# A hybrid decoder trunk on one core: small tensors laid down first, large SBUF buffers at multiples of 512 bytes

## The chip, the cores and the metric

One core of one Trainium2 chip runs the whole program. The metric is the device time of one execution in microseconds; lower is better. One execution was also taken with the hardware profiler, and its rows are read below.

## The reference

```python
D_MODEL, SEQ, DEPTH, D_FF = 1024, 512, 2, 4096
def hybrid_layer(x, g_mix, w_in, w_a, w_b, w_o, g_ffn, w_up, w_down):
    proj = rmsnorm(x, g_mix) @ w_in       # 1024 x 9728
    qa, ka, va, qr, kr, vr, gr, ga, gb = jnp.split(proj, SPLIT_POINTS, axis=-1)
    ...   # rotary; three groups of windowed attention with dilation 1, 4, 16, 8 heads of 64 each
    wts = jax.nn.softmax(jnp.stack(lses, axis=0), axis=0)
    y_a = (sum over the groups of wts * outs) @ w_a
    ret = retention(qr, kr, vr)           # 4 heads, keys 128, values 256, decay per head
    y_b = (silu(gr) * rms-normed ret) @ w_b
    x = x + (sigmoid(ga) * y_a + sigmoid(gb) * y_b) @ w_o
    x = x + square(relu(rmsnorm(x, g_ffn) @ w_up)) @ w_down
    return x
```

Two such layers and a last RMSNorm; everything is float32, batch 1.

## The kernel before, in words

**Layout.** Activations lie transposed: 128 features on the partitions, the 512 positions along the free dimension, so `x` is 128 x 8 x 512. Weights come as units of 128 x 2048 float32 (1 MB), two buffers of each kind.

**Three products.** A float32 product is made of three matmuls in the fp32r format. Each operand is split into a high part (a cast) and a low part (the difference): high x high, high x low, low x high, all summed in one PSUM bank (`three`, L1073 to L1077). The moving operand of these, 512 columns of 4 bytes, is the activation (`h_hi`, `h_lo`; `z_hi`, `z_lo`; `m_hi`, `m_lo`; `y_hi`, `y_lo`; in the MLP's second half `u_hi`, `u_lo`, which are `z_hi`, `z_lo` by another name, L159). The weights are the stationary operand. For the values the roles are turned round: the activations are stationary and the weights move, 512 columns at L1124 to L1126 (groups 1 and 2 read `h` with a step of 4, `by_residue`), 256 columns at L1234 to L1236.

**Who splits.** SyncE loads `w_raw` (L305), ScalarE casts it to `w_hi` (L393), VectorE subtracts to `w_lo` (L683), in halves of 1024 columns. TensorE waits for the count of `lo_done`. A unit of weights feeds 48 matmuls.

**Order of a layer.** Values of the three attention groups (six units, 288 matmuls a layer); then a loop over four pairs of heads; in each, three units of queries and keys with rotary (ACT copies out, POOL multiplies by the cosines into `rcos`, L663; DVE shuffles, multiplies and adds, L766 to L779), then twelve steps in which TensorE puts a slice of a projection between the small float32 matmuls of attention and retention: `scores` (L1161), `turn` (L1171), `values` (L1184), `st` (L1197), `ret` (L1210). At the end of a pair DVE makes `z`: `silu` (L822, L827), the square root on ACT (L544), a reciprocal (L856) and two products (L861, L864); its next instructions are the next pair's `w_lo`. Then four passes over the gates (L914, L926) with `w_b` and `w_a`, `w_o` in four units, and the MLP in four chunks of four units `w_up` and four units `w_down`. The waits are semaphores, written out by hand on each engine.

**SBUF.** `sb` takes the next free address, rounded up to 32 bytes. Before the kernel's own tensors the partition is in use up to byte 16481. `x`, `h_hi`, `h_lo`, `w_raw`, `w_hi`, `w_lo`, `tables`, `rstd_all`, `decay`, `mask` come first, then the small ones (L105 to L117). Above them, from `zone0` (L120), lie zones that share the same bytes at different times: "P" for the pairs, "G" for gates and merge, "N" for the norms and the MLP, "X" and "Y" for input and output; `at` (L123) places a tensor. `other` (L115) receives the softmax statistics of the other order by DMA in `exchange` (L345 to L358) and is read in `factors` (L882). `nmax` and `den` (L145, L146) are written by `masked` and `exp` and copied into `stats` in `u_copy` (L795).

Of the kernel before, what the change touches and what calls it, by code (L numbers as in the profile page):

```python
# [35 lines left out]
P = 128  # L36
F32 = mybir.dt.float32
# [14 lines left out]
def trunk(nc, a):  # L52
    S = a["x"].shape[1]
    D = a["x"].shape[2]
    DEPTH = a["w_in"].shape[0]
    KT = D // P
    TB = S // P
# [4 lines left out]
    HEADS = 2 * PAIRS  # L62
# [20 lines left out]
    with ExitStack() as ctx:  # L83
        def sb(name, shape, dt):
            return ctx.enter_context(nc.sbuf_tensor(name, shape, dt))
# [5 lines left out]
            return ctx.enter_context(nc.semaphore(name))  # L91


        x = sb("x", [P, KT, S], F32)
        h_hi = sb("h_hi", [P, KT, S], F32R)
        h_lo = sb("h_lo", [P, KT, S], F32R)
# [4 lines left out]
        cosA, sinA, cosR, sinR = (tables[:, i, :] for i in range(4))  # L101
        rstd_all = sb("rstd_all", [P, S], F32)
        decay = sb("decay", [P, S], F32)
        mask = sb("mask", [P, S], F32)
        ident = sb("ident", [P, P], F32)  # L105
        ones = sb("ones", [P, P], F32)
        inv_d = sb("inv_d", [P, 1], F32)
        gains = sb("gains", [P, 2 * DEPTH + 1, KT], F32)
        gain = sb("gain", [P, 2, KT], F32)
        std = sb("std", [P, 2 * TB], F32)  # L110
        rstd = sb("rstd", [P, 2 * TB], F32)
        eps = sb("eps", [P, 1], F32)

        stats = sb("stats", [P, 2 * TB, 2, HEADS], F32)
        other = sb("other", [P, 2 * TB, 2, HEADS], F32)  # L115
        tick = sb("tick", [P, 1], F32)
        warm = sb("warm", [P, 1], F32)  # L117


        zone0 = -(-nc.sbuf_base // 64) * 64  # L120
        top = {}

        def at(scope, name, shape, dt):  # L123
            off = top.get(scope, zone0)
            n = 2 if dt == BF16 else 4
            for d in shape[1:]:
                n *= d
            top[scope] = off + -(-n // 32) * 32
            return nc.alloc_sbuf_tensor_at(name, shape, dt, offset=off)
# [12 lines left out]
        swp = at("P", "swp", [P, S], F32)  # L142
        rcos = at("P", "rcos", [P, S], F32)
        silu = at("P", "silu", [P, 2, S], F32)
        nmax = at("P", "nmax", [P, 2 * TB, 2], F32)  # L145
        den = at("P", "den", [P, 2 * TB, 2], F32)  # L146

        m_hi = at("G", "m_hi", [P, KT, S], F32R)
        m_lo = at("G", "m_lo", [P, KT, S], F32R)
# [1228 lines left out]
```

## Time and profile before

| | us |
|---|---|
| median of 3 runs | 2015.46 |
| lowest, highest | 2014.9, 2018.23 |
| the profiled execution | 2016.15 |
| its span | 2014.3 |
| TensorE busy, share of the span | 99% |
| VectorE, ScalarE, GpSimd busy | 55%, 36%, 5% |
| mean busy share of the 16 DMA engines | 27.8% |
| mean granted clock of TensorE | 0.998 |

The span runs from the first to the last instruction of the program. In the rows, PE is TensorE's matmul, PEld its weight load (which overlaps the matmuls), DVE VectorE, ACT ScalarE, POOL GpSimd. A matmul's end is modelled: neighbours overlap in the rows, so the time that one takes in a stream is the distance between two starts.

### The profile page before, as it was taken

The numbers are of one execution on the slowest core, as the hardware profiler recorded it, in microseconds if no ns is written. First come the engines' busy times: TensorE is split into PE (matmuls) and PEld (weight loads), VectorE is DVE, ScalarE is ACT, GpSimd is POOL, SyncE is SP. The second block draws the span as 40 slices with busy tenths as digits, with TensorE's granted clock in tenths as the row PEclk, the third lists the DMA queues.
The fourth block names the chain that finished last, engine by engine and source line by source line (L and its number), as shares of the span: only waits on it lengthen the run. The fifth ranks groups of instructions, "written<-read, shape, count | busy, mean of one in ns | idle before, by whom it ended". The sixth has DMA issues, their size and how long they took to land.

```text
span 2014.3 us, 27151 instructions
## 1 busy us (share of the span) xinstructions
PE 1987.7 (99%) x9640; PEld 1656.1 (82%) x9640; DVE 1108.2 (55%) x1724; ACT 727.5 (36%) x1147; POOL 98.2 (5%) x71
## 2 busy tenths in 40 slices
PE   8999999999999999999999999999999999999999
PEld 7988888888888888888889888888888888888887
DVE  5466574747446635444635574757564565445355
ACT  4143535354223313223322534344432233223233
POOL 0010110200000000000001110202000000000000
PEclk9999999999999999999999999999999999999999
DMA  5321222212223233232333222213133323232321
GB/s 173 106 90 48 83 89 62 89 44 84 94 94 105 84 104 101 87 104 84 105 106 89 63 89 62 89 42 99 44 95 97 111 84 105 84 104 83 104 84 63
DMA packets 202544, 177.63 MB, mean 88 GB/s; under 512 B 8432, under 2 KB 192880, under 8 KB 202224
## 3 DMA queue, kind: packets, MB, share of 16 engines
q1 hardware_dynamic: 202192, 176.51, 27.8%
q8 instruction: 38, 0.62, 0.1%
q10 hardware_dynamic: 288, 0.28, 0.0%
q14 instruction: 26, 0.21, 0.0%
HBM read 174.54 MB, written 2.23 MB: 88 GB/s over the span
## 4 chain that ended last, share of the span: by engine, by line
PE 75%; DVE 14%; issue 7%; ACT 2%; POOL 1%; DVEq 0%; DMA 0%; ACTq 0%; POOLq 0%; SPq 0%
PE pj L1075 19%; PE pj L1077 19%; PE pj L1076 19%; DVE w_lo L683 4%; DVE swp L768 3%; PE yo L1184 2%; DVE swp L766 2%; PE rb L1210 2%; DVE probT L856 1%; PE pj L1234 1%; PE pj L1236 1%; PE pj L1235 1%; PE pt L1171 1%; PE sc L1124 1%; PE sc L1126 1%
## 5 line engine op out<-in xcount | busy, mean ns | idle before, releaser
L1075 PE MATMUL pj<-h_hi,w_hi 128*128 128x512 f32 x1408 | 558.2, 396 | 2.2 <-DVE sA L914 1.6
L1077 PE MATMUL pj<-h_hi,w_lo 128*128 128x512 f32 x1408 | 548.6, 390 | 0.0
L1076 PE MATMUL pj<-h_lo,w_hi 128*128 128x512 f32 x1408 | 548.4, 389 | 0.0
L393 ACT CAST w_hi<-w_raw 128x1024 fp32r<-128x1024 f32 x330 | 329.0, 1045 | 380.1 <-PE pj L1077 286.1
L683 DVE TENSOR_TENSOR w_lo<-w_raw,w_hi 128x1024 fp32r<-128x1024 f32 x330 | 404.4, 1267 | 82.7 <-ACT w_hi L393 82.0
L1075 PEld LDWEIGHTS pj<-h_hi,w_hi 128*128 128x128 f32 x1408 | 264.4, 188 | 61.8 <-DVE w_lo L683 5.5
L1077 PEld LDWEIGHTS pj<-h_hi,w_lo 128*128 128x128 f32 x1408 | 264.3, 188 | 56.1
L1076 PEld LDWEIGHTS pj<-h_lo,w_hi 128*128 128x128 f32 x1408 | 264.5, 188 | 54.9 <-issue 1.8
L1075 PE MATMUL pj<-z_hi,w_hi 128*128 128x512 f32 x640 | 252.6, 395 | 0.6 <-DVE sB L914 0.6
L1077 PE MATMUL pj<-z_hi,w_lo 128*128 128x512 f32 x640 | 252.2, 394 | 0.0
L1076 PE MATMUL pj<-z_lo,w_hi 128*128 128x512 f32 x640 | 252.2, 394 | 0.0
L978 DVE TENSOR_TENSOR x<-pj,x 128x512 f32<-128x512 f32 x80 | 55.2, 691 | 201.4 <-PE pj L1077 201.4
L663 POOL TENSOR_TENSOR rcos<-rot,tables 128x512 f32<-128x512 f32 x64 | 97.7, 1526 | 1307.1 <-ACT rot L465 1175.9
L1075 PEld LDWEIGHTS pj<-z_hi,w_hi 128*128 128x128 f32 x640 | 119.7, 187 | 30.3 <-issue 1.1
L1077 PEld LDWEIGHTS pj<-z_hi,w_lo 128*128 128x128 f32 x640 | 119.7, 187 | 29.8
L1076 PEld LDWEIGHTS pj<-z_lo,w_hi 128*128 128x128 f32 x640 | 119.7, 187 | 29.3
L992 DVE TENSOR_TENSOR relu<-relu,rstd_all 128x512 f32<-128x512 f32 x64 | 44.3, 692 | 90.4 <-ACT relu L607 89.8
L465 ACT COPY rot<-pj 128x512 f32<-128x512 f32 x48 | 28.2, 587 | 182.1 <-PE pj L1077 96.8
L476 ACT ACTIVATE prob<-prob,nmax 128x256 f32<-128x256 f32 (+1 forms) x128 | 62.4, 489 | 66.0 <-DVE nmax L790 65.6
L607 ACT ACTIVATE relu<-pj 128x512 f32<-128x512 f32 x64 | 38.3, 599 | 129.2 <-PE pj L1077 129.2
L1234 PE MATMUL pj<-w_hi,h_hi 128*128 128x256 f32 x256 | 79.4, 310 | 0.0
L790 DVE CUSTOM_DVE_ANT_0 prob<-sc,mask 128x256 f32<-128x256 f32 (+1 forms) x128 | 46.9, 404 | 56.6 <-issue 56.6
(185 smaller groups left out, 2358.1 us busy)
## 6 DMA issues: line engine op xcount, KB each, us to landing
w_raw<-in_w_in SPq DMA_DIRECT2D x152, 512.0 KB, 4.4
w_raw<-in_w_up SPq DMA_DIRECT2D x64, 512.0 KB, 4.4
w_raw<-in_w_down SPq DMA_DIRECT2D x64, 512.0 KB, 4.3
w_raw<-in_w_b SPq DMA_DIRECT2D x16, 512.0 KB, 4.0
w_raw<-in_w_o SPq DMA_DIRECT2D x16, 512.0 KB, 4.0
w_raw<-in_w_a SPq DMA_DIRECT2D x16, 256.0 KB, 3.0
x_nat<-in_x SPq DMA_DIRECT2D x2, 1024.0 KB, 7.0
tables<-in_tables SPq DMA_DIRECT2D x2, 1024.0 KB, 6.8
```

The lines of the kernel that those rows point to most:

```text
L393: nc.scalar.copy(w_hi[s][:, c], raw[s][:, c]).then_inc(hi_done, 1)
L476: nc.scalar.activation(prob[:, c], prob[:, c], ACT.Exp, scale=-1.0, bias=nmax[:, at_, b % 2:b % 2 + 1], accum_out=den[:, at_, b % 2:b % 2 ...
L663: nc.gpsimd.tensor_tensor(rcos[:], rot[:], cosA if u < 3 else cosR, ALU.mult).then_inc(rot_cos, 1)
L683: nc.vector.tensor_tensor(w_lo[s][:, c], raw[s][:, c], w_hi[s][:, c], ALU.subtract).then_inc(lo_done, 1)
L768: nc.vector.tensor_tensor(swp[:], swp[:], sinA if u < GROUPS else sinR, ALU.mult).then_inc(rot_sin, 1)
L790: nc.vector.tensor_tensor_reduce(out=prob[:, c], in0=sc[:, (b % 2) * S + c.start:(b % 2) * S + c.stop], in1=mask[:, c], scale=-(DH ** -0.5 ...
L978: nc.vector.tensor_tensor(x[:, t, :], pj[o][:], x[:, t, :], ALU.add).then_inc(bank_free[o], 1)
L992: nc.vector.tensor_tensor(relu2[:, o, :], relu[:, o, :], rstd_all[:], ALU.mult).then_inc(relu_scaled, 1)
L1075: nc.tensor.matmul(out, w_hi[s][:, wc], acts[0], start=first, stop=False)
L1076: nc.tensor.matmul(out, w_hi[s][:, wc], acts[1], start=False, stop=False)
L1077: return nc.tensor.matmul(out, w_lo[s][:, wc], acts[0], start=False, stop=last)
L1234: nc.tensor.matmul(out, hh, w_hi[sl][:, w], start=(k == 0), stop=False)
```

## The change

The small tensors are allocated first; a filler brings the next address to a multiple of 512; `zone0` is rounded up to 512 instead of 64. `other` is no longer a tensor of its own but a view of `decay`'s first 128 columns. `nmax` and `den` move from the zone "P" to the small tensors. No instruction, wait or order changes on any engine.

```diff
+        ident = sb("ident", [P, P], F32)
+        ones = sb("ones", [P, P], F32)
+        inv_d = sb("inv_d", [P, 1], F32)
+        gains = sb("gains", [P, 2 * DEPTH + 1, KT], F32)
+        gain = sb("gain", [P, 2, KT], F32)
+        std = sb("std", [P, 2 * TB], F32)
+        rstd = sb("rstd", [P, 2 * TB], F32)
+        eps = sb("eps", [P, 1], F32)
+
+        stats = sb("stats", [P, 2 * TB, 2, HEADS], F32)
+        tick = sb("tick", [P, 1], F32)
+        warm = sb("warm", [P, 1], F32)
+        nmax = sb("nmax", [P, 2 * TB, 2], F32)
+        den = sb("den", [P, 2 * TB, 2], F32)
+
+        fill = -nc.sbuf_base % 512
+        if fill:
+            sb("fill", [P, fill // 4], F32)
         x = sb("x", [P, KT, S], F32)
...
         decay = sb("decay", [P, S], F32)
+        other = decay[:, 0:2 * TB * 2 * HEADS].rearrange("p (b w h) -> p b w h", b=2 * TB, w=2)
         mask = sb("mask", [P, S], F32)
-        ident = sb("ident", [P, P], F32)
...
-        other = sb("other", [P, 2 * TB, 2, HEADS], F32)
...
-        zone0 = -(-nc.sbuf_base // 64) * 64
+        zone0 = -(-nc.sbuf_base // 512) * 512
...
-        nmax = at("P", "nmax", [P, 2 * TB, 2], F32)
-        den = at("P", "den", [P, 2 * TB, 2], F32)
```

## Rows read from the trace of the kernel before

**Rows 1.** The page, parts 1 and 2: busy time of each engine, granted clock.
```profile
PE 1987.7 (99%) x9640; PEld 1656.1 (82%) x9640; DVE 1108.2 (55%) x1724; ACT 727.5 (36%) x1147; POOL 98.2 (5%) x71
...
PEclk9999999999999999999999999999999999999999
```

**Rows 2.** Waits of PE: us in total, times, the longest.
```profile
PE sc L1047 <- DMA x_nat<-in_x: 7.2, 1, 7.2
PE rb L1197 <- DVE qkR L779: 5.3, 8, 0.7
```

**Rows 3.** Timeline, PE, moving `h`: start us, duration us, instruction.
```profile
1500.05 0.39 PE L1075 MATMUL pj<-h_hi,w_hi 128*128 128x512 f32 x1
...
1505.04 0.39 PE L1076 MATMUL pj<-h_lo,w_hi 128*128 128x512 f32 x1
```

**Rows 4.** Timeline, PE, moving `z`.
```profile
1505.49 0.39 PE L1075 MATMUL pj<-z_hi,w_hi 128*128 128x512 f32 x1
...
1511.79 0.39 PE L1075 MATMUL pj<-z_hi,w_hi 128*128 128x512 f32 x1
```

**Rows 5.** Groups by line and form: count, busy us, mean ns, idle before.
```profile
L1075 PE MATMUL pj<-h_hi,w_hi 128*128 128x512 f32 x1408 | 558.2, 396 | 2.2 <-DVE sA L914 1.6
...
L1076 PEld LDWEIGHTS pj<-h_lo,w_hi 128*128 128x128 f32 x1408 | 264.5, 188 | 54.9 <-issue 1.8
...
L1075 PE MATMUL pj<-z_hi,w_hi 128*128 128x512 f32 x640 | 252.6, 395 | 0.6 <-DVE sB L914 0.6
...
L1075 PE MATMUL pj<-m_hi,w_hi 128*128 128x512 f32 x128 | 50.4, 394 | 0.0
```

**Rows 6.** Timeline, PE, moving `w` with 256 columns.
```profile
315.90 0.28 PE L1234 MATMUL pj<-w_hi,h_hi 128*128 128x256 f32 x1
...
318.30 0.28 PE L1236 MATMUL pj<-w_hi,h_lo 128*128 128x256 f32 x1
```

**Rows 7.** Windows: stretch, length, PE, PEld, DVE, ACT, POOL busy, clock, DMA share, GB/s.
```profile
670.00:1000.00 330.00, 330.00 (x1436) 268.67 (x1435) 164.68 (x200) 103.27 (x135) 0.00 (x0) 1.00 0.30 96
...
30.40:32.60 2.20, 2.20 (x7) 1.68 (x6) 2.00 (x7) 2.19 (x4) 0.00 (x0) 0.50 0.17 20
```

**Rows 8.** Timeline, PE, group 0's values, in the second stretch of rows 7.
```profile
30.44 0.63 PE L1125 MATMUL sc<-w_lo,h_hi 128*128 128x512 f32 x1
...
32.57 0.63 PE L1124 MATMUL pt<-w_hi,h_hi 128*128 128x512 f32 x1
```

**Rows 9.** Timeline, PE, float32 matmuls of `ret`, starts of two neighbours.
```profile
166.04 0.59 PE L1210 MATMUL rb<-ST,vR 128*128 128x512 f32 x1
...
166.47 0.59 PE L1210 MATMUL rb<-ST,vR 128*128 128x512 f32 x1
```

**Rows 10.** Timeline, PE, values of a group that reads `h` with a step.
```profile
59.81 0.40 PE L1126 MATMUL sc<-w_hi,h_lo 128*128 128x512 f32 x1
...
61.93 0.40 PE L1126 MATMUL yo<-w_hi,h_lo 128*128 128x512 f32 x1
```

**Rows 11.** Timeline, PE, a pair's middle; in brackets the idle time before.
```profile
314.36 1.15 PE L1161 MATMUL sc<-qk 64*128 64x256 f32 x12
...
325.53 1.10 PE L1197 MATMUL rb<-qkR 128*128 128x512 f32 x2 [0.66 <-DVE qkR L779]
```

**Rows 12.** Chain that ended last, a pair's end: start us, us, what.
```profile
356.32 0.70 DVE silu L822
...
368.01 1.17 DVE w_lo L683
```

**Rows 13.** The page, part 6, DMA issues: count, KB each, us to landing.
```profile
x_nat<-in_x SPq DMA_DIRECT2D x2, 1024.0 KB, 7.0
tables<-in_tables SPq DMA_DIRECT2D x2, 1024.0 KB, 6.8
```

**Rows 14.** Groups by line and form, ACT's casts of 512 columns.
```profile
L415 ACT CAST h_hi<-hn 128x512 fp32r<-128x512 f32 x40 | 24.3, 608 | 2.6 <-DVE hn L690 2.0
...
L612 ACT CAST z_hi<-relu 128x512 fp32r<-128x512 f32 x64 | 39.8, 621 | 100.1 <-DVE relu L994 100.1
```

More of the change, by code:

```diff
@@ L103, in trunk @@
         decay = sb("decay", [P, S], F32)
+        other = decay[:, 0:2 * TB * 2 * HEADS].rearrange("p (b w h) -> p b w h", b=2 * TB, w=2)
         mask = sb("mask", [P, S], F32)
-        ident = sb("ident", [P, P], F32)
[L106 to L114, printed above, removed]
-        other = sb("other", [P, 2 * TB, 2, HEADS], F32)
-        tick = sb("tick", [P, 1], F32)
-        warm = sb("warm", [P, 1], F32)
-        zone0 = -(-nc.sbuf_base // 64) * 64
+        zone0 = -(-nc.sbuf_base // 512) * 512
         top = {}
```

## The prediction

> **What bounds the kernel now.** I read the page's first two parts first. TensorE (PE) is busy 99% of the span and its granted clock stays at the top level in every slice [rows 1]; VectorE (DVE) at 55% and ScalarE (ACT) at 36% are far behind. Then the waits of PE: the largest are 7.2 us for the first input and 5.3 us, in eight pieces, for `qkR` [rows 2], and all the others together come to less than 9 us. So the time is the number of matmuls times their spacing, and the question is what sets the spacing.
>
> The busy time can't say it (a pipelined matmul shows 390 ns), so I took starts from the timeline. Three products of one form, 128x512 in fp32r, at the same full clock, differ by where the moving operand lies. In the compiled kernel before, `x` begins at byte 16512 of the partition, 128 above a multiple of 512, and since the sizes of everything down to `mask` are multiples of 512, so do `h_hi`, `h_lo`, `w_hi`, `w_lo`. The small tensors end at 131588, so `zone0` is 131648, 64 above a multiple of 512, and so are `z_hi`, `z_lo`, `m_hi`, `m_lo`, `y_hi`, `y_lo`.
> - Moving `h` (start 128): 22 intervals from 1500.05 to 1505.04 us are 226.8 ns each [rows 3], which is 544 cycles of 2.4 GHz: 512 columns and 32 more.
> - Moving `z` (start 64), the same weights as stationary operand: 27 intervals from 1505.49 to 1511.79 are 233.3 ns each [rows 4]: 560 cycles, 48 more. `m` shows the modelled duration of `z`, 394 and 395 ns [rows 5], and `y` lies as they do.
> - Moving `w_hi`, `w_lo` with 256 columns (start 128): 20 intervals from 315.90 to 318.30 are 120.0 ns each [rows 6]: 288 cycles, again 32 more, at half the length. The extra belongs to the start, not to the length.
>
> A whole stretch bears the two out: 330 us of the MLP, where `h` and `z_hi`, `z_lo` take turns, hold 1436 matmuls, 229.8 ns each, the mean of 226.7 and 233.3 [rows 7].
>
> Both extras follow from one rule: if PE is fed in blocks of 256 bytes (64 columns of 4 bytes), a stream that starts inside a block must take its last block whole. From 64, 2048 bytes end 64 bytes into a block: (2304-64)/4 = 560. From 128: (2304-128)/4 = 544. From 128 with 1024 bytes: (1280-128)/4 = 288. A start on a boundary adds nothing. Two more rows speak for a limit of the supply and not of PE: at the low clock (granted 0.50, 1.2 GHz [rows 7]) five intervals of the 512-column form with `w` at start 128 take 2.13 us, 426 ns or 511 cycles, without an extra [rows 8]; and the fp32 form, which takes two cycles a column, takes 430 ns for 512 columns with `ST` at start 64, 6 cycles over 1024 [rows 9].
>
> **The change part by part.**
> *Large buffers.* After the change the small tensors take 16512 to 18592, the filler 352 bytes, `x` starts at 18944 = 37 x 512 and `zone0` is 131584 = 257 x 512. So every moving operand of the 1-cycle products starts on a boundary. Price of one aligned 512-column matmul: bounds are 213.3 ns (512 cycles) and 240 ns (below, a rival); I take 215.8 ns, 518 cycles, since [rows 9] shows 6 cycles over the columns where the supply can't be the limit. The weight load of 188 ns [rows 5] fits under it.
> The Trainium skill (TensorE: Matmul & The Clock Gate, Back-to-back issue gap) gives 512/2.4 + about 2.5, measured 215.7 ns, for this size in bf16. The rows here are 11 and 18 ns above it; by it the sum would come out as mine.
> Counts: `h` 3 x 1408 = 4224; `z` and `m` 3 x (640+128) [rows 5] and `y` 3 x 64 by the loops, 2496 together.
> - `h`: 4224 x (226.7 - 215.8) = 46.0 us.
> - `z`, `m`, `y`: 2496 x (233.3 - 215.8) = 43.7 us.
> - Values for attention (L1124 to L1126, moving `w`, 576 in all by the loops): the 192 of group 0 save 10.9 ns each, 2.1 us. The 384 of the other groups load `h` with a step of 4; nine intervals take 235.6 ns [rows 10], more than the 226.7 of group 0's kind, so I take that load as their limit and save nothing. Bound: 384 x 19.8 = 7.6 us.
> - 256 columns (L1234 to L1236), 768: 120.0 to 262/2.4 = 109.2, 8.3 us.
> Sum 100.1 us.
>
> *What of it is lost.* Each of the eight pairs has two stretches where DVE, ACT and POOL chains end last, so a faster PE only waits longer. First, from the scores at 314.4 to `st` at 325.5: PE already sits idle 0.66 us for `qkR` [rows 11]; the 48 matmuls of 256 columns beside that chain save 0.52 us that becomes waiting. Second, the end of the pair: `silu` at 356.32, then the sigmoid, the square root, a reciprocal, the products for `z`, and `w_lo` at 368.01 [rows 12]; PE runs the next pair's first unit (48 matmuls) beside it and is about caught up, so another 0.52 us goes. Smaller waits in the attention steps may keep 0.2 more, a guess from these two. So 1.25 us of the 3.65 that a pair could give, 10 us in all, and 1 us at the start and at the gates. In the MLP nothing is lost: a unit of 48 matmuls goes from 11.0 to 10.4 us, DVE is busy there half the time, ACT 31%, the DMA engines 30% [rows 7]. Net 100 - 11 = 89 us.
>
> *DMA.* Landings into `w_raw` move from start 128 to 0. PE never waits for one except `x_nat` at the start [rows 2]. Of two 1 MB transfers, `tables` (start 128) lands in 6.8 us, `x_nat` (start 64) in 7.0 [rows 13]: 0.2 us at most; I take nothing. No DMA is added, none passes another, and no wait is added.
> *ACT and DVE.* The same cast takes 608 ns into `h_hi` and 621 into `z_hi` [rows 14]: a difference of 13 ns under PE's cover, and in the lossy stretches at most some tens of ns per pair. Nothing.
> *`other` inside `decay`, `nmax` and `den` out of the zone.* The same instructions on other addresses. `decay` was last read in the layer's fourth pair, before the exchange, and is loaded again after the next layer's values. Nothing.
>
> The profiled execution took 2016.15 us with a span of 2014.3; the median of the runs is 2015.46. From the median: 2015.5 - 89 = 1926.5, say 1927 us.
>
> **Rivals.**
> *Other floors of the same rule.* No residue at all (213.3 ns): 7680 matmuls save 2.5 ns more, 19 us, of which 2 are lost: 1909 us. A residue of 16 cycles (220 ns, 113.3 for 256 columns): 28.2 + 33.3 + 1.3 + 5.1 = 68, less 7: 1954 us.
> *32 cycles are a fixed cost* and only the 64-byte start costs more. All would run at 226.7: 2496 x 6.7 = 16.6 us, 1999 us. For it: 32 is the least extra that a row shows at full clock. Against: [rows 8].
> *Start addresses don't matter* (the change doesn't do what it says). `z`, `m`, `y` also lie above 131072, so the 16 cycles could be of the place, with 32 fixed: 2015.5 us. The Trainium skill (SBUF — State Buffer, Door 1) says that reads run at full bandwidth with two or more hits in each 16-byte line; all starts here are multiples of 16, so by it nothing would change. Against: no row shows 512 or 518 cycles at full clock, and 560, 544 and 288 come from one formula without a constant.
> *Slower.* The same three rows also fit "extra = columns up to the next boundary, and a start on one pays a full block": 48 at 64, 32 at 128, 64 at 0. Then a matmul takes 576 cycles, 240 ns: 4224 x 13.3 + 2496 x 6.7 + 192 x 13.3 + 384 x 4.4 + 768 x 13.3 = 87 us more, 2103 us. It decides from an aligned spacing of 229 ns on, the mean of today's. Against: it needs a block fetched for nothing.
>
> **Chances.** Forecast 0.60, the floors 213.3 and 220 0.10 each, 226.7 0.07, no effect 0.06, slower 0.07. The range 1905 to 1965 holds the first three with their bounds (values 7.6 us, losses between 4 and 16 us). A change below 0.2%, 4 us, is not told from none here. Faster 0.87, same 0.06, slower 0.07.
>
> **What would show it.** In the profile after: `h` and `z` timelines with one spacing, near 216 ns; 256 columns near 109; a unit of 10.4 us; the MLP stretch some 6% shorter; larger idle times before `qkR`'s matmul and before the second unit of a pair; fp32 products and every DVE and ACT mean as before. Spacings of 226.7 or 240 for `h` would make it wrong, as would an unchanged sum with new idle time in the MLP.

## The result, and the profile after

The changed kernel takes 1998.62 us in the median of 4 runs (1997.93 to 2001.2), against 2015.18 us for the kernel before (the three runs of the table and a fourth, 2014.14): a ratio of 0.9918, with a 95% interval of 0.9901 to 0.9935. It is faster by 16.6 us. Forecast was 1927 with a range of 1905 to 1965; the sign was right, the size was wrong by a factor of five. The rival with 1999 us had a chance of 0.07.

The page of the changed kernel, part 1 and a row of part 6 [rows 1, 13]. All lines of the kernel's body are 4 higher than before.

```profile
PE 1969.5 (99%) x9640; PEld 1656.4 (83%) x9640; DVE 1108.3 (56%) x1724; ACT 727.8 (36%) x1147; POOL 98.0 (5%) x71
...
x_nat<-in_x SPq DMA_DIRECT2D x2, 1024.0 KB, 6.4
```

Its timeline of PE where `h` gives way to `z`, as [rows 3, 4]:

```profile
1492.11 0.39 PE L1079 MATMUL pj<-h_hi,w_hi 128*128 128x512 f32 x1
...
1495.51 0.39 PE L1079 MATMUL pj<-z_hi,w_hi 128*128 128x512 f32 x1
...
1498.91 0.39 PE L1079 MATMUL pj<-z_hi,w_hi 128*128 128x512 f32 x1
```

Fifteen intervals each: 3.40 us and 3.40 us, 226.7 ns. `z` came down from 233.3; `h` did not move at all. The forms that carry the sum [rows 5], and the MLP [rows 7]:

```profile
L1079 PE MATMUL pj<-h_hi,w_hi 128*128 128x512 f32 x1408 | 558.2, 396 | 2.2 <-DVE sA L918 1.6
...
L1079 PE MATMUL pj<-z_hi,w_hi 128*128 128x512 f32 x640 | 249.3, 390 | 0.7 <-DVE sB L918 0.7
```

```profile
670.00:992.00 322.00, 322.00 (x1423) 266.70 (x1422) 162.46 (x197) 101.28 (x131) 0.00 (x0) 1.00 0.30 98
...
1000.50:1003.50 3.00, 3.00 (x9) 2.29 (x8) 0.34 (x2) 1.09 (x1) 0.00 (x0) 0.53 0.02 5
```

`h` has the busy time of before to the tenth. In each layer, from the first matmul that moves `z` to the layer's end (in the second layer to the end of the program), the trace shows 538.1 and 549.3 us before, 530.1 and 540.6 after: 16.7 us, which is 2496 x 6.7 ns. The loops over the pairs take 345.1 and 345.0 before, 345.2 and 345.2 after. The two spans differ by 18.2 us: the 16.7, 0.6 by which PE waits less for `x_nat`, and about 1.7 for a stretch of 3.4 us at the low clock (granted 0.5), of which the execution before has one more than this one; the wait for `w_lo`, which grows from 1.8 to 2.4 us, takes 0.6 of it back.

Where it waits [rows 2]:

```profile
PE sc L1051 <- DMA x_nat<-in_x: 6.6, 1, 6.6
PE rb L1201 <- DVE qkR L783: 5.3, 8, 0.7
```

### The profile page after: what moved, and what is told of

Read it like the earlier page. It is cut to its first block, busy times and chain, and to the rows that moved or that the text cites. A ratio compares the mean times of both kernels' runs of the same rounds, so it can differ in the third digit from the quotient of the medians.

```text
span 1996.1 us, 27151 instructions
## 1 busy us (share of the span) xinstructions
PE 1969.5 (99%) x9640; PEld 1656.4 (83%) x9640; DVE 1108.3 (56%) x1724; ACT 727.8 (36%) x1147; POOL 98.0 (5%) x71
## 4 chain that ended last, share of the span: by engine, by line
PE 75%; DVE 14%; issue 7%; ACT 2%; POOL 1%; DVEq 0%; DMA 0%; ACTq 0%; POOLq 0%; SPq 0%
PE pj L1079 19%; PE pj L1081 19%; PE pj L1080 19%; DVE w_lo L687 4%; DVE swp L772 3%; PE yo L1188 2%; DVE swp L770 2%; PE rb L1214 2%; DVE probT L860 1%; PE pj L1238 1%; PE pj L1240 1%; PE pj L1239 1%; PE pt L1175 1%; PE sc L1128 1%; PE rb L1201 1%
## 5 line engine op out<-in xcount | busy, mean ns | idle before, releaser
L1081 PEld LDWEIGHTS pj<-z_hi,w_lo 128*128 128x128 f32 x640 | 120.2, 188 | 24.9
```

Source lines behind the costliest of these rows:

```text
L1081: return nc.tensor.matmul(out, w_lo[s][:, wc], acts[0], start=False, stop=last)
```

## The experiments

Two theories stood after the result. *Own start*: what counts is where the moving operand starts, in units of 128 bytes; 32 cycles are fixed. *Difference*: what counts is the start of the moving operand minus that of the stationary one. Before, `h` and `w` both lay at 128 and `z` at 64 against `w` at 128; no row had told the two apart.

### Three layouts of the whole kernel

`e1_zone_128`, the kernel before with one line changed:

```diff
-        zone0 = -(-nc.sbuf_base // 64) * 64
+        zone0 = -(-nc.sbuf_base // 128) * 128
```

> The kernel before with one edit: zone0 is rounded up to a multiple of 128 instead of 64, so z, m and y start 128 above a multiple of 512, as the main group does; nothing else moves. Own start (unit 128) and difference of the starts both say: z, m, y at 226.7 ns, 16.6 us less than before, 1998.6 us, the whole gain of the change. If a start at a multiple of 256 or 512 is needed, z, m, y stay at 233.3 and the time at 2015.

2001.55 us, ratio 0.9923 (0.9906 to 0.9939). `z` is back at the busy time that it has in the changed kernel, and at a spacing of 226.7 ns:

```profile
L1075 PE MATMUL pj<-z_hi,w_hi 128*128 128x512 f32 x640 | 249.4, 390 | 0.6 <-DVE sB L914 0.6
```

The gain of the change is this line's: neither 512 nor laying the small tensors down first is needed for it. The median is 2.9 us above the changed kernel's, which goes with the granted clock: three of the four runs have a mean of 0.997, and the one at 0.999 took 1998.52 us. Both theories live.

`e2_all_64`, the changed kernel moved as a whole:

```diff
-        fill = -nc.sbuf_base % 512
+        fill = (64 - nc.sbuf_base) % 512
...
-        zone0 = -(-nc.sbuf_base // 512) * 512
+        zone0 = -(-nc.sbuf_base // 64) * 64
```

> The changed kernel with everything large moved by 64 bytes: main group and zone both start 64 above a multiple of 512. Own start (unit 128): every 1-cycle product pays 16 cycles more than in the changed kernel, h too: 233.3 ns for h, z, m, y, 126.7 for the 256 columns; 16.6 us for z, m, y and 28.2 + 1.3 + 5.1 us for the rest, of which the waits of the pairs take up some 5: about 2045 us. Difference of the two starts: moving and stationary operands agree, so all stay at 226.7 and the time at 1999 us.

1999.57 us, ratio 0.9920 (0.9903 to 0.9936). All starts of large buffers are 64 above a multiple of 512, where `z` had cost 233.3 before, and the rows are those of the changed kernel:

```profile
L1079 PE MATMUL pj<-h_hi,w_hi 128*128 128x512 f32 x1408 | 558.1, 396 | 2.2 <-DVE sA L918 1.6
...
L1079 PE MATMUL pj<-z_hi,w_hi 128*128 128x512 f32 x640 | 249.4, 390 | 0.8 <-DVE sB L918 0.8
```

Own start falls here.

`e3_main_64`, the changed kernel with the same `fill` with 64 and `zone0` rounded up to 128, so that `z` lies 128 above a multiple of 512 and its weights 64:

> The changed kernel with the main group (x, h, w, tables) 64 above a multiple of 512 and the zone 128 above one. Own start (unit 128): h and the moving weights pay 16 cycles more, z, m, y don't: h at 233.3, z at 226.7, about 1999 + 30 = 2029 us. Difference of the starts: h (64) against w (64) stays at 226.7, z (128) against w (64) goes to 233.3, 2015 us.

2007.03 us, ratio 0.9956 (0.9940 to 0.9973), which neither theory had named. `h` stays at 226.7, as the difference says; `z` goes up, but to 229.2 in the mean (232.2, 226.2 and 229.3 ns by the three products) and not to 233.3. So a difference of +64 is not one of -64, and the blocks below give its price.

### Blocks of matmuls by themselves

`m1_starts` and `m2_differences` leave the trunk out: PE runs blocks of 48 or 96 matmuls of one form, all on zeros,

```python
for k in range(N):
    mm = nc.tensor.matmul(ps[0][:, 0:512], W(0, 128, k), M(d, 512, k), start=(k == 0), stop=(k == N - 1))
```

where `W(s, ...)` starts s bytes and `M(d, ...)` d bytes above a multiple of 512.

> The trunk is left out; the output is zeros. TensorE alone runs 31 blocks of 48 matmuls from SBUF into one bank each, every block with another start of the moving or the stationary operand, width or type. Read is the spacing of starts inside a block at full clock. Own start (unit 128): a moving start of 0, 128, 256, 384 gives 226.7 ns for 512 columns of fp32r, one of 16, 32, 64, 96, 192, 320, 448 gives 233.3, whatever the stationary start. Difference of the two starts: 226.7 where both have the same start modulo 128, so also with both at 64 or both at 32, and 233.3 where they differ, so also with moving 0 and stationary 64. The 32 cycles that are left at start 0: if they are paid by each matmul as such, 64 or 32 stationary columns and one stationary tile used again and again still take 226.7; if they are the cost of the stationary columns, 64 columns give 528 cycles, 220.0 ns, and 32 columns 520, 216.7. bf16 with 512 columns: 216 to 220 if the residue is of the 4-byte type, 226.7 if it is of every matmul.

> The trunk is left out; the output is zeros. Blocks of 96 matmuls in fp32r; the stationary operand starts at 0 modulo 512, the moving one at d. Theory: the cost depends on the difference d modulo 256 alone. 512 columns: 544 cycles (226.7 ns) at d = 0 and 256, about 549 at 64, 560 at 32, 96, 128, 192, 224; open is whether 8, 48, 80, 112, 144, 160, 176, 208, 240 lie between or below. If one of them is below 544, a layout with that difference beats both kernels. 256 columns: 288 cycles at 0, 283 at 64. The 32 cycles left at d = 0: if they come from weight reads and moving reads that meet in SBUF, they go (to 512 to 518 cycles, 213 to 216 ns) when the moving operand is one column read again and again (step 0), or the stationary one is; if each fp32r matmul pays them as such, the step 0 blocks stay at 226.7 ns. Stationary operand with a step of 4 (as in the values of groups 1 and 2): 235 ns whatever d, if the load is the limit; else it moves with d.

The mean spacing from the first to the last start of a block, fp32r, 512 columns, 128 stationary ones; where both runs have a value they agree within 0.2 ns, except at 128 (233.4 and 232.4); each block was run once in a run:

| moving minus stationary, bytes | ns | cycles |
|---|---|---|
| 0, 240, 256 | 226.7 to 227.1 | 544 to 545 |
| 64, 320 | 228.8, 229.2 | 549, 550 |
| 16, 80, 112, 176 | 231.1 to 231.7 | 555 to 556 |
| 128, 384 | 232.4 to 233.4 | 558 to 560 |
| 8, 32, 48, 96, 144, 192, 224, 448 | 233.2 to 233.6 | 560 to 561 |
| 160, 208 | 234.2, 234.7 | 562, 563 |
| moving 0, stationary 32, 64, 128, 256 | 233.2, 233.4, 232.5, 226.8 | |
| both 32, both 64, both 128 | 227.5, 227.6, 227.6 | |
| 256 columns: 0, 64, 128, 192 | 119.9, 117.8, 118.7, 113.7 | 288, 283, 285, 273 |
| stationary with a step of 4: 0, 64, 128, 192 | 237.8, 239.9, 239.6, 238.3 | |
| moving: one column, step 0 | 215.8 | 518 |
| stationary: one column, step 0 | 228.9 | 549 |
| bf16, moving 0, 64, 128 | 216 (median) | 518 |

To within 1 ns, only the difference modulo 256 counts, and none of the differences tried is better than 0 for 512 columns and 128 stationary ones. Two things that `m1_starts` expected fell: a difference of 128 costs as much as one of 192 (the period is 256, not 128), and 64 or 32 stationary columns take 229.9 and 231.7 ns, neither 220.0 and 216.7 nor 226.7. One stationary tile used again and again takes 227 ns (median in `m1_starts`; 227.0, with the moving tile repeated too, in `m3_residue`). In the groups of `m2_differences` (count, busy, mean ns; the spacing is (busy - mean)/95), the differences 0, 64 and 192, then one moving column:

```profile
L83 PE MATMUL ps<-mov,sta 128*128 128x512 f32 x96 | 21.9, 389 | 0.0
...
L98 PE MATMUL ps<-mov,sta 128*128 128x512 f32 x96 | 22.1, 391 | 0.0
...
L122 PE MATMUL ps<-mov,sta 128*128 128x512 f32 x96 | 22.6, 394 | 0.0
...
L173 PE MATMUL ps<-mov,sta 128*128 128x512 f32 x96 | 20.9, 379 | 0.0
```

The last row is what I had put as the price of an aligned matmul: 518 cycles. PE can do it; a stream of 512 different columns of 4 bytes didn't, at any of the starts tried.

`m3_residue` asks where the other 26 to 32 cycles come from.

> The trunk is left out; the output is zeros. Blocks of 96 fp32r matmuls about the 32 cycles that stay at difference 0 and go when the moving operand is one column (518 cycles). If they come from how many different addresses the moving stream reads: a run of 4, 8, 16, 64, 128 or 256 columns read again until 512 are made shows from which length they return, and 128 columns read 4 times each stand near 518. If they come from meetings with the weight loads: narrower loads (96, 64, 32 columns) need fewer cycles at some difference, in proportion, and each width has its own best difference. Lengths 320, 384, 448, 480: 352, 417, 480, 512 cycles if the residue is 32 per matmul and no share of the length.

Each of 128 columns read four times in a row: 518 cycles; a run of 4 columns again and again 518, of 8 columns 520; of 64, 128 or 256 columns 544, as the full stream; of 16 columns 581. Narrower stationary operands don't help: over the differences 0, 64, 128, 192, 96 columns take 552, 560, 556, 548 cycles, 64 take 552, 548, 550, 558, and 32 take 554 to 556. That goes against a cost in proportion to the width of the weight load. But each width has its cheapest difference elsewhere, as was expected if the moving stream meets the weight loads; for 96 and 64 columns it isn't 0. Lengths: 352 cycles for 320, 416 for 384, 486 for 448, 520 for 480. So 480 columns cost 40 more than their number and 512 only 32: neither a fixed price nor a share. How many different columns the moving stream reads has a part in it; that it meets the weight loads is argued from the differences, and how stays open.

`m4_low_clock` lets PE stand still before each block; its blocks have 96 matmuls, not the 48 of the text on record.

> The trunk is left out; the output is zeros. TensorE stands still for over 15 us before each of seven blocks of 48 fp32r matmuls, so that each block begins at the low clock. If the extra cycles come from how fast SBUF feeds TensorE at 2.4 GHz, then at 1.2 GHz every difference (0, 64, 128, 192, 32) takes 427 ns for 512 columns and 213 for 256, without an extra; if they are cycles of TensorE, 453 ns at difference 0 and 467 at 192.

The windows of the block with difference 192 (granted clock 0.50, then 1.00), and starts in its timeline:

```profile
157.00:160.00 3.00, 3.00 (x9) 2.32 (x8) 0.00 (x0) 0.00 (x0) 0.00 (x0) 0.50 0.00 0
165.00:175.00 10.00, 10.00 (x45) 8.01 (x44) 0.00 (x0) 0.00 (x0) 0.00 (x0) 1.00 0.01 2
```

```profile
156.33 1.22 PE L107 MATMUL ps<-mov,sta 128*128 128x512 f32 x2 [22.10 <-ACT tick L53]
...
159.48 1.05 PE L107 MATMUL ps<-mov,sta 128*128 128x512 f32 x2
...
163.76 0.63 PE L107 MATMUL ps<-mov,sta 128*128 128x512 f32 x2
...
173.79 0.39 PE L107 MATMUL ps<-mov,sta 128*128 128x512 f32 x1
```

From 156.33 to 159.48 there are seven intervals, the first of 595 ns, the others of 426 to 427; from 163.76 to 173.79 forty-three, 233.3 each. After each block's first intervals, the low clock shows 426 to 427 ns at every difference tried (0, 64, 128, 192, 32) and 213 to 214 for 256 columns (differences 0 and 192): no extra. A cost in PE's own cycles would have been there at either clock; so this is a limit outside them that only the full clock meets, as [rows 8] had suggested.

### Two more differences and a moved weight buffer

> The changed kernel with the zone 64 above a multiple of 512 and the main group at 0, so z, m, y move at a difference of +64 to their weights (before it was -64). Difference theory: 228.8 ns for them as in the blocks, 2496 x 2.2 = 5.4 us more than the changed kernel, 2004 us. A rule of the moving operand's own start (64 costs 16 cycles): 233.3 ns and 2015 us.

```diff
-        zone0 = -(-nc.sbuf_base // 512) * 512
+        zone0 = -(-nc.sbuf_base // 512) * 512 + 64
```

2007.96 us, ratio 0.9958 (0.9941 to 0.9975). `z` lies at 64 as in the kernel before, and yet takes 229.2 ns, with the three values of `e3_main_64`: about 6 us more than the changed kernel. The rest of the 9.3 goes with the low clock: its profiled execution has four stretches at it while PE works, that of the changed kernel one (each has another after PE's last matmul, which costs nothing).

> The changed kernel with the zone 128 above a multiple of 512 and the main group at 0: difference +128. Difference theory: 232.4 ns for z, m, y, 2496 x 5.8 = 14.4 us more than the changed kernel, 2013 us. By its own start, z at 128 cost no more than 226.7 ns in the kernel whose zone and main group both lay at 128: 1999 us.

The same edit with + 128: 2015.58 us, ratio 0.9996 (0.9987 to 1.0006). `z` takes 233.4 to 233.5 ns (the blocks had 233.4 and 232.4), 2496 x 6.7 = 16.7 us: the whole gain is gone, with `z` at the start that cost nothing in `e1_zone_128`. Seventeen intervals of its timeline:

```profile
1509.83 0.40 PE L1081 MATMUL pj<-z_hi,w_lo 128*128 128x512 f32 x1
...
1513.80 0.39 PE L1080 MATMUL pj<-z_lo,w_hi 128*128 128x512 f32 x1
```

> The changed kernel with a pad of 64 bytes between the activations and the weight buffers, the zone at a multiple of 256: all activations start at 0, all weights 64 later (difference -64 modulo 256). Difference theory: h too goes to 233.3 ns: 4224 x 6.7 = 28.2 us and 2496 x 6.7 = 16.6 us more than the changed kernel, the moving weights (difference +64) change by less than 2 us together, the pairs take up 1 to 4 us in their waits: 2039 to 2042 us. Own start of the moving operand: all activations at 0, 1999 us.

```diff
         h_lo = sb("h_lo", [P, KT, S], F32R)
+        sb("pad", [P, 16], F32)
...
-        zone0 = -(-nc.sbuf_base // 512) * 512
+        zone0 = -(-nc.sbuf_base // 256) * 256
```

2040.9 us, ratio 1.0124 (1.0107 to 1.0140): 64 bytes ahead of the weights make the kernel 42.3 us slower than the changed one in the medians, though every activation starts at a multiple of 256. `h` and `z` are both at 233.3 to 233.5 ns. Its groups:

```profile
L1080 PE MATMUL pj<-h_hi,w_hi 128*128 128x512 f32 x1408 | 565.5, 402 | 1.1 <-DVE sA L919 1.1
...
L1080 PE MATMUL pj<-z_hi,w_hi 128*128 128x512 f32 x640 | 252.7, 395 | 0.1
```

A part of the 42.3 is the clock. The profiled executions, both at a mean of 0.999, took 2035.25 and 1997.93 us, 37.3 us apart, and the latter has in it 1.7 us for a low-clock stretch that the other doesn't have. So the layout costs some 39 us, the low edge of what was expected. The products' 45 us are not all seen, since the pairs take up some in their waits, and the other runs, at 0.996 and 0.997, carry more low clock.

### A layout from the table

The table has 113.7 ns for 256 columns at a difference of 192. `e7_values_192` gives just these products that difference. ACT and DVE write this unit's `w_hi` and `w_lo` 48 columns (192 bytes) later, in buffers made longer for it, with all large buffers at multiples of 256; PE reads them there (one line of the edit):

```diff
-                                w = slice(k * 256, k * 256 + 256)
+                                w = slice(48 + k * 256, 48 + k * 256 + 256)
```

> The changed kernel unchanged, beside the next one on the same chip: 1998 to 2001 us; its runs differ from each other by the stretches at the low clock, some 1.7 us each.

> The changed kernel; the weights of the retention's values (the 768 products of 256 columns, in which the weights move and h stands still) are written 192 bytes later in their buffers, which grow by 256 bytes; everything large starts at a multiple of 256. Difference theory: 113.7 ns instead of 119.9 for the 256 columns, as in the blocks with d = 192, 768 x 6.2 = 4.8 us; half of them lie beside the chain to st and only lengthen the wait for qkR, so 2.4 us less than the changed kernel, 1996 us. All other spacings as in the changed kernel, since multiples of 256 do as well as 512. If the blocks of 48 between other work don't fall into the same rhythm as the blocks of 96, no difference, 1998.6 us.

The changed kernel beside it: 1999.31 us (1998.22 to 2001.02). `e7_values_192`: 1999.91 us (1995.59 to 2000.47); the ratios to the kernel before, 0.9920 and 0.9913, have intervals that overlap, so no gain is shown in the medians. In the trace the spacing in the blocks fell from 117 to 120 ns to 113 to 119. The three lines' spacings sum to 3.0 us less, and a part of it comes back as the wait for `qkR`, 6.2 us instead of 5.3:

```profile
PE rb L1202 <- DVE qkR L784: 6.2, 8, 0.8
```

The loops over the pairs take 344.1 and 344.1 us instead of 345.2 and 345.2. Those 2.2 us are hidden in the total by stretches at the low clock, four while PE works in its profiled execution against two in its neighbour's. One of them, as the windows show it in this kernel; the changed kernel holds its clock at this place:

```profile
654.00:657.50 3.50, 3.50 (x10) 2.82 (x11) 1.32 (x5) 0.27 (x1) 0.00 (x0) 0.52 0.74 262
```

Runs with the same mean clock point to a gain, though they are few: 1995.59 against 1998.22 us at 0.999, 1999.71 to 2000.47 against 2000.95 and 2001.02 at 0.997.

## Why the prediction was wrong

**The bound.** Right: the time is the number of matmuls times their spacing. PE is busy 99%, waits are as before, and every layout's time follows from the spacings and the stretches at the low clock.

**The rule, the step that failed.** "Both extras follow from one rule: if PE is fed in blocks of 256 bytes ... A start on a boundary adds nothing." It fitted 560, 544 and 288 cycles, but these three were two observations: difference 0 costs 32 cycles at both lengths, and difference -64 costs 48. The start of the moving operand and its difference to the stationary one were never told apart in the rows, because the weights lay at one residue throughout. The rule's own argument, "one formula without a constant", counted the same fact twice. `e2_all_64` parts them. The period of 256 was right, for the difference.

**Large buffers, `h`.** 46.0 us forecast, 0 measured: its difference was 0 before and after. The 8.3 us of the 256 columns (121.7 ns before, 121.6 after in the mean of the three lines) and 2.1 of the values: 0, for the same reason. The other 384 values, whose stationary operand has a step of 4, were rightly put at nothing: their form takes 237.8 to 239.9 ns at every difference tried. **`z`, `m`, `y`.** 43.7 us forecast, 16.7 measured (6.7 ns instead of 17.5). **The price of an aligned matmul.** This term was mis-sized too: 215.8 ns was taken from the 6 cycles of the fp32 form, whose moving operand is read at half the rate; at one new column a cycle no start and no difference tried gives it. 226.7 is what it measured. The same 226.7 was the least that the trace before held for this form at the full clock, and I set it aside for a row at half the rate and a row at half the clock. Both spoke for a limit of supply, which `m4_low_clock` bears out; neither showed that a good address removes it.

**What is lost in the pairs.** 10 us forecast, nothing there to lose, since nothing in a pair became faster. The mechanism shows in `e7_values_192`: of 3.0 us that the 256 columns save, 0.9 turn into waiting for `qkR`.

**DMA.** "I take nothing" for `x_nat`: PE waits 6.6 us instead of 7.2.

**Rivals.** The one at 1999 us had the right time and the 32 cycles at every address in the kernel. Its reasons did not hold: that a start at 64 costs more fell with `e2_all_64`, and the 32 cycles are no fixed cost either, since 480 columns pay 40 and one repeated column 6. The floor at 32 deserved more than 0.07: it was the only price that a row showed. "Start addresses don't matter" was half true: moving everything together changes nothing, and moving one group does. The slower rival fell: `h` at a boundary takes 226.7, not 240. That a layout can be slower than the one before was shown by `e5_weights_64`, 24.9 us in the medians, by another mechanism.

**Two figures of pages.** The gap of 512/2.4 + about 2.5 ns, some 216 (the Trainium skill, TensorE: Matmul & The Clock Gate, Back-to-back issue gap), agrees with the bf16 blocks here, 216, and with fp32r on one repeated column, 215.8. It does not hold for a streamed fp32r operand, 226.7 at best. The rule of 16-byte lines (the Trainium skill, SBUF — State Buffer, Door 1) would, as the prediction read it, make all these layouts equal; they differ by some 39 us (42 in the medians), and the measurement decides.

## What to carry to other kernels

For fp32r matmuls of 512 columns against 128 stationary ones, on a core that PE bounds, let moving and stationary operands start at the same address modulo 256. Where both lie hardly matters (under 1 ns), and 64 bytes between them cost 2.1 to 2.5 ns a matmul when the moving operand lies later and 6.7 when it lies earlier. Other shapes have another best difference: 192 for 256 columns, 192 or 64 for 96 or 64 stationary ones; measure yours. Read the spacing of starts for each shape, since busy times of pipelined matmuls hide it. And before a cost is put down to one operand's address, look for a row in which the other operand's address differs too; if none exists, the price of the least row is the forecast and the rule is a rival.

## What was not expected

- An fp32r stream at the full clock takes 544 cycles for 512 columns at best. At a difference of 0 it takes 520 for 480, 416 for 384 and 288 for 256 (273 at a difference of 192). At 1.2 GHz, 512 and 256 columns take no extra at all.
- A run of 16 columns read again and again is slower than 512 different ones, 581 cycles.
- DMA landings go a little with the SBUF address: `w_raw` from `w_in`, `w_up`, `w_o` takes 4.2 to 4.3, 4.2 and 3.8 to 3.9 us in the five kernels where it starts at a multiple of 256, and 4.4 to 4.5, 4.3 to 4.5 and 3.9 to 4.1 in the five where it starts at 64 or 128 above one. `x_nat` takes 6.3 to 6.4 us in the four whose zone starts at a multiple of 256 and 6.6 to 7.0 in the other six. But for `w_down` the ranges overlap (4.0 to 4.2 and 4.0 to 4.3), and `tables` shows nothing (6.9 to 7.2 and 6.8 to 7.2). The Trainium skill (DMA: Bandwidth & Descriptors, How a descriptor splits into AXI transactions) says that a descriptor which doesn't start at a multiple of 256 bytes has its first transaction start at the boundary below it, and that the bytes before the start are fetched and still cost beats; the rows of `w_in` and `x_nat` are in line with that, but no run here isolates it.
- In the traces of the whole kernel PE's clock falls to 1.2 GHz for stretches of 3.4 us (once 6.8), each after a wait of some 2 us or after sixteen matmuls of one column, or after PE's last one, and from execution to execution at other such places. A stretch of 3.4 us with matmuls in it costs about 1.7, half its length. The spread of 3 to 4 us between runs of one kernel goes with their mean clock: 1998.22 us at 0.999, 2001.02 at 0.997.
